# Eight modulation rows and the mixer's sums of squares as TensorE columns, gates by tanh, the mixer's work in new orders

## The chip, the cores and the metric

One core of a Trainium2 chip runs the whole network. The metric is the device time of one execution in microseconds (us), lower is better. Engines are named as in the profile: PE is TensorE (PEld its weight loads), DVE is VectorE, ACT is ScalarE, POOL is GpSimd, SP is the queue that issues DMAs.

## What is computed

Two layers over 512 tokens of width 1024, in float32. Each layer computes six modulation vectors of a conditioning vector `c` (48 rows of 128 results per layer), a mixer (sliding-window attention beside a gated linear recurrence) and a gated feed-forward part (FFN) with a short convolution.

```python
def rg_lru(x, w_a, b_a, w_x, b_x, lam):
    r = sigmoid(einsum('bsnd,nde->bsne', xb, w_a) + b_a)
    i = sigmoid(einsum('bsnd,nde->bsne', xb, w_x) + b_x)
    log_a = -LRU_C * r * softplus(-lam)
    a = exp(log_a)
    b = sqrt(-expm1(2.0 * log_a)) * (i * x)
    _, h = associative_scan(combine, (a, b), axis=1)
    return h

c_act = silu(c)
for l in range(DEPTH):
    mod = (c_act @ ada_w[l] + ada_b[l]).reshape(bsz, N_MOD, D_MODEL)
    shift_m, scale_m, gate_m, shift_f, scale_f, gate_f = ...
    h = rms_norm(x, mix_pre_g[l]) * (1.0 + scale_m) + shift_m
    # mixer: q, k, v, x_lru, gate = split(h @ w_in[l]); attention; rg_lru
    merged = concatenate([rms_norm(attn_out, g_attn), rms_norm(lru_out, g_lru)])
    x = x + gate_m * rms_norm(merged @ w_out[l], mix_post_g[l])
    h = rms_norm(x, ffn_pre_g[l]) * (1.0 + scale_f) + shift_f
    x = x + gate_f * rms_norm(conv_ffn(h, ...), ffn_post_g[l])
```

## The kernel before

Activations lie transposed: 128 features by 512 tokens a tile. Each engine has its own program, written out in order, and they meet at semaphores.

**Weights.** A product with a weight chunk (128 outputs, 1024 inputs, 512 KB) takes three passes: `ACT` copies the raw chunk to its high part `wH` (`split_step`, line 558), DVE subtracts to get the low part `wL` (`lo_chunk`, line 1089), and PE adds up high by high, high by low and low by high (line 1833). Six chunks are held in a ring. A chunk's load is issued on SP (line 430) when PE has finished the chunk six places before (`chunk_done`).

**The in-projection.** The first six chunks of a layer (k, four q, v) are done by token halves in one group (`first_group` in layer 0, `next_group` in layer 1). Chunks 6 to 13 (four x for the recurrence, four gate) follow as `tile_products` of 24 passes on 128x512 each. Between their halves (`midway`) and behind them (`behind`) PE does the attention's and the recurrence's small products: `scores_mm`, `values`, `gates`, `probs_transposed`, `outputs_mm`, each for one of four blocks of tokens or channels.

**The out-projection.** `half_products` with the attention's half of the inputs (chunks O0 to O0+5, both token halves, 12 passes of 128x256 a chunk and half), the norm's statistics, and then the recurrence's half. Attention and recurrence outputs are each normed: `square_out` and `out_squares` (line 1318) square the attention output and sum it over four tiles on DVE, `lru_square` and `lru_sum` (line 1373) do so for the recurrence, and `norm_cols` turns the sums over partitions into columns of a PSUM bank on PE, with the data as weights and a column of ones as the moving operand. `sd_step`, the reciprocals and `norm_spread` make the scale, and `lru_scaled`, `lru_high`, `lru_low` (lines 1527, 758, 1533) apply it before PE can start on the recurrence's half.

**Modulation rows.** A row is a *unit*: a 512 KB tile of `ada_w`, multiplied by the broadcast `csb` and summed along the free axis by one DVE instruction (`dot_unit`, line 1095, counted in `ada_used`). Units 0 to 15 are done before the in-projection, four of them (`PE_SHIFT`) as eight one-column products on PE (`shift_sums`). Units 16 to 23 (`IN_UNITS`, the gate of the mixer) are done by DVE inside layer 0's mixer, units 24 to 39 (`late`) from the end of the mixer through the out-projection, and 40 to 95 in layer 0's FFN, one or two behind a weight chunk's `lo_chunk` (`UNITS`). Their loads are issued by SP (line 444), in one program with the weight loads: for each such unit SP waits until DVE has used the one that lies in its slot, and goes on to the next weight load only then.

```python
if l == 0 and i in UNITS and not NPROJ <= i < FFN0:
    for u in UNITS[i]:
        unit_refill(unit_after(u), u)
```

**Gates.** `gate_sigmoids` (lines 705, 706) uses the sigmoid, `decays` (lines 712, 715) exp and tanh, so ACT loads function tables between them.

The order of the mixer's steps is written out by hand for each engine and layer (the lists from lines 796 on ACT, 1385 on DVE and `midway`/`behind` on PE). An fp32 product of small operands (columns, scores, gates) is one instruction in the program and stands as two rows in the trace.

Of the kernel before, what the change touches and what calls it, by code (L numbers as in the profile page):

```python
# [25 lines left out]
P = 128  # L26
DEPTH, SEQ, D = 2, 512, 1024
# [64 lines left out]
PE_SHIFT = (1, 3, 5, 7)  # L92
SLAB = GRP * P
# [4 lines left out]
def build(nc, A):  # L98
# [3 lines left out]
    with ctx:  # L102
# [51 lines left out]
        tiny = sb("tiny", [P, 132])  # L154
# [33 lines left out]
        presq = [scr[:, :], vwf, work[:, :], gw[:, :, :].rearrange("p a b -> p (a b)")]  # L188
        ada_slots = [stage[:, 10, :], stage[:, 11, :], adaw[:, 0, :], adaw[:, 1, :], vwf]
# [67 lines left out]
        sdx, rsx = tiny[:, 124:128], tiny[:, 128:132]  # L257
        edge = sb("edge", [P, GRP, BACK])
        nil = sb("nil", [P, P], fp32r)
# [9 lines left out]
        ada_used = sem("ada_used")  # L269
        csil_ready, csil_mm, csb_ready = sem("csil_ready"), sem("csil_mm"), sem("csb_ready")  # L270
# [11 lines left out]
        lru_summed = sem("lru_summed")  # L282
# [14 lines left out]
        gate_mm, sig_done, aT_ready, b2_ready = sem("gate_mm"), sem("sig_done"), sem("aT_ready"), sem("b2_ready")  # L297
# [3 lines left out]
        pt_mm, pt_copied, o_mm, o_copied, osq_ready = sem("pt_mm"), sem("pt_copied"), sem("o_mm"), sem("o_copied"), sem("osq_ready")  # L301
# [95 lines left out]
        IN_UNITS = range(2 * KT, 3 * KT)  # L397
        LATE_UNITS = range(3 * KT, DEPTH * NMOD * KT)
# [4 lines left out]
        def unit_fill(u):  # L403

            return sum(1 for v in range(2 * KT, u + 1) if unit_slot(v) == unit_slot(u))

        def unit_after(u):

            return u + 3 if u + 3 < LATE_UNITS.stop else None


        @block.sync
        def _(sp):
# [29 lines left out]
            def ada_fill(u):  # L443
                sp.dma_start(ada_slots[unit_slot(u)], A["ada"][u]).then_inc(ada_in[unit_slot(u)], 16)

            def unit_refill(u, before):

                if u is not None:
                    sp.wait_ge(ada_used, UNIT0 + before - 2 * KT + 1)
                    ada_fill(u)  # L450
# [1920 lines left out]
```

## Time and profile before

| | |
|---|---|
| median of 3 runs | 1223.01 us (1222.08 to 1223.96) |
| the profiled execution: its own time | 1217.96 us |
| its span | 1216.1 us |
| its mean granted TensorE clock | 0.975 |
| PE busy | 1165.7 us, 96% |
| PEld busy | 1010.2 us, 83% |
| DVE busy | 864.0 us, 71% |
| ACT busy | 545.4 us, 45% |
| POOL busy | 13.1 us, 1% |

Times in the trace count from the start of the span. Layer 0's mixer runs from 54 to 205 us, its FFN to 640, layer 1's mixer from there to 791, its FFN to the end. A granted clock of 1.00 is 2.4 GHz, 0.50 is 1.2 GHz. Line numbers in profile rows are those of the kernel before.

### The profile page before, as it was taken

How to read it: one execution, taken by the hardware profiler on the slowest of the kernel's cores; microseconds unless marked ns; L12 is line 12 of the kernel's file. 1: busy time of each engine (PE TensorE's matmuls, PEld its weight loads, DVE VectorE, ACT ScalarE, POOL GpSimd, SP SyncE). 2: the span in 40 equal slices, each digit the busy share in tenths (PEclk: the TensorE clock that was granted, in tenths of full speed). 3: DMA queues.
4: the chain of work that ended last, by engine and by line, in shares of the span. 5: the costliest groups of instructions: out<-in, count | busy, mean ns of one | idle time of the engine just before them, and what ended most of it. 6: DMA issues, size and time to landing. Idle time of an engine off the chain costs nothing.

```text
span 1216.1 us, 16091 instructions
## 1 busy us (share of the span) xinstructions
PE 1165.7 (96%) x6588; PEld 1010.2 (83%) x6588; DVE 864.0 (71%) x1337; ACT 545.4 (45%) x775; POOL 13.1 (1%) x35
## 2 busy tenths in 40 slices
PE   7989888999899999999999999999999999999995
PEld 7977688988788888888999778988888888888895
DVE  8899988778876777777586997478753656346645
ACT  5579634454324431444346894435531444134430
POOL 4000000000000000000000000000000000000000
PEclk8999988999999999999999999989999999999998
DMA  9632547044684448643222221303333323333212
GB/s 359 232 103 71 190 142 240 1 156 164 219 281 166 150 139 268 222 156 111 83 68 89 69 70 53 105 1 123 103 95 96 104 87 104 91 100 103 88 53 70
DMA packets 44937, 155.78 MB, mean 128 GB/s; under 512 B 5056, under 2 KB 7360, under 8 KB 44864
## 3 DMA queue, kind: packets, MB, share of 16 engines
q1 hardware_dynamic: 44720, 154.23, 38.2%
q8 instruction: 52, 0.85, 0.3%
q10 hardware_dynamic: 144, 0.52, 0.1%
q14 instruction: 21, 0.17, 0.0%
HBM read 152.64 MB, written 2.10 MB: 127 GB/s over the span
## 4 chain that ended last, share of the span: by engine, by line
PE 78%; DVE 12%; DMA 4%; ACT 3%; issue 2%; SPq 1%; DVEq 0%
PE ps L1833 77%; DMA sb_stage<-in_ada 2%; DVE sb_wL L1089 2%; DMA sb_raw<-in_w 2%; DVE sb_R L1559 1%; DVE sb_y L1148 1%; ACT sb_R L778 1%; DVE sb_adaw L1095 1%; DVE sb_x L1152 1%; DVE sb_y L1170 1%; DVE sb_y L1358 1%; ACT sb_hH L605 0%; DVE sb_mL L1380 0%; DVE sb_ssqv L1318 0%; DMA sb_vw<-in_ada 0%
## 5 line engine op out<-in xcount | busy, mean ns | idle before, releaser
L1833 PE MATMUL ps<-sb_hH,sb_wH 128*128 128x512 f32 (+1 forms) x1184 | 424.7, 364 | 7.7 <-ACT sb_hH L605 5.2
L1833 PE MATMUL ps<-sb_hH,sb_wL 128*128 128x512 f32 (+1 forms) x1184 | 418.2, 359 | 0.0
L1833 PE MATMUL ps<-sb_hL,sb_wH 128*128 128x512 f32 (+1 forms) x1184 | 395.1, 358 | 2.7 <-DVE sb_hL L1177 2.7
L1833 PEld LDWEIGHTS ps<-sb_hH,sb_wH 128*128 128x128 f32 x1184 | 228.8, 193 | 43.5 <-ACT sb_hH L605 6.0
L1833 PEld LDWEIGHTS ps<-sb_hH,sb_wL 128*128 128x128 f32 x1184 | 228.7, 193 | 31.7
L1833 PEld LDWEIGHTS ps<-sb_hL,sb_wH 128*128 128x128 f32 x1184 | 214.0, 192 | 35.5 <-DVE sb_hL L1177 3.3
L558 ACT ACTIVATE sb_wH<-sb_raw 128x1024 fp32r<-128x1024 f32 x174 | 181.5, 1050 | 138.3 <-DMA sb_raw<-in_w 138.1
L1089 DVE TENSOR_TENSOR sb_wL<-sb_raw,sb_wH 128x1024 fp32r<-128x1024 f32 x174 | 211.4, 1219 | 38.3 <-ACT sb_wH L558 38.1
L1833 PE MATMUL ps<-sb_mH,sb_wH 128*128 128x256 f32 (+1 forms) x608 | 207.0, 341 | 3.7 <-ACT sb_mH L992 3.5
L1833 PE MATMUL ps<-sb_mL,sb_wH 128*128 128x256 f32 (+1 forms) x608 | 205.9, 339 | 1.7 <-DVE sb_mL L1533 1.7
L1833 PE MATMUL ps<-sb_mH,sb_wL 128*128 128x256 f32 (+1 forms) x608 | 205.3, 338 | 0.0
L1833 PEld LDWEIGHTS ps<-sb_mH,sb_wH 128*128 128x128 f32 x608 | 118.2, 194 | 16.5 <-ACT sb_mH L992 4.0
L1833 PEld LDWEIGHTS ps<-sb_mL,sb_wH 128*128 128x128 f32 x608 | 118.2, 194 | 14.8 <-DVE sb_mL L1533 2.5
L1684 DVE SCALAR_TENSOR_TENSOR sb_R<-ps,sb_par,sb_R 128x511 f32<-128x511 f32 x84 | 62.9, 748 | 94.9 <-ACT sb_R L986 94.8
L1833 PEld LDWEIGHTS ps<-sb_mH,sb_wL 128*128 128x128 f32 x608 | 118.2, 194 | 11.4
L986 ACT ACTIVATE sb_R<-ps,sb_par 128x512 f32<-128x512 f32 x84 | 65.2, 776 | 103.9 <-PE ps L1833 103.9
L992 ACT ACTIVATE sb_mH<-sb_I 128x512 fp32r<-128x512 f32 x42 | 26.5, 632 | 100.7 <-DVE sb_I L1694 100.7
L1687 DVE SCALAR_TENSOR_TENSOR sb_R<-ps,sb_par,sb_R 128x510 f32<-128x510 f32 x84 | 62.9, 748 | 3.0
L1095 DVE SCALAR_TENSOR_TENSOR sb_adaw<-sb_adaw,sb_csb 128x1024 f32<-128x1024 f32 x48 | 57.9, 1219 | 4.9 <-DMA sb_adaw<-in_ada 4.5
L1696 DVE TENSOR_TENSOR sb_mL<-sb_I,sb_mH 128x512 fp32r<-128x512 f32 x42 | 29.1, 692 | 29.3 <-ACT sb_mH L992 29.3
L982 ACT ACTIVATE sb_I<-sb_R 128x512 f32<-128x512 f32 x42 | 26.6, 632 | 49.1 <-DVE sb_R L1687 49.1
L605 ACT ACTIVATE sb_hH<-sb_y,sb_mod 128x256 fp32r<-128x256 f32 x48 | 22.8, 503 | 28.1 <-DVE sb_y L1170 28.0
(223 smaller groups left out, 1098.3 us busy)
## 6 DMA issues: line engine op xcount, KB each, us to landing
sb_raw<-in_w SPq DMA_DIRECT2D x174, 512.0 KB, 3.7
sb_adaw<-in_ada SPq DMA_DIRECT2D x48, 512.0 KB, 4.4
sb_stage<-in_ada SPq DMA_DIRECT2D x24, 512.0 KB, 11.2
sb_vw<-in_ada SPq DMA_DIRECT2D x24, 512.0 KB, 4.6
sb_side<-in_w SPq DMA_DIRECT2D x8, 512.0 KB, 4.9
sb_raw<-in_w SPq DMA_DIRECT2D x8, 384.0 KB, 14.6
sb_x<-in_x SPq DMA_DIRECT2D x4, 512.0 KB, 5.3
out<-sb_x SPq DMA_DIRECT2D x4, 512.0 KB, 2.9
```

Of the source, the lines that this page charges most:

```text
L558: nc.scalar.activation(high_of(n), raw_of(n), ACT.Copy).then_inc(w_hi, 1)
L605: nc.scalar.activation(hH[:, j, part_of(h)], yt(j)[:, part_of(h)], ACT.Identity, bias=bias[:, j:j + 1], scale=1.0).then_inc(hi_ready, 1)
L778: last = nc.scalar.activation(R[:, c % 4, part_of(h)], pair_bank(h, p)[:, (c % 2) * HALF:(c % 2 + 1) * HALF], ACT.Identity, bias=pcol(l, " ...
L982: nc.scalar.activation(I[:, p % 2, :], R[:, (c - 1) % 4, :], ACT.Gelu_apprx_tanh).then_inc(f_gelu, 1)
L986: nc.scalar.activation(R[:, c % 4, :], bank(up_bank(u)), ACT.Identity, bias=par_l[:, COLS["fcb"] + col:COLS["fcb"] + col + 1], scale=pcol( ...
L992: nc.scalar.activation(mH[:, p, :], I[:, 2 + p % 2, :], ACT.Copy).then_inc(act_hi, 1)
L1089: TT(low_of(n), raw_of(n), high_of(n).bitcast(fp32), ALU.subtract).then_inc(w_lo, 1)
L1095: STT(out=tile, in0=tile, scalar=1.0, in1=csb[:, :], op0=ALU.mult, op1=ALU.mult, accum_out=mod[:, seg, kt:kt + 1]).then_inc(ada_used, 1)
L1684: link(STT(out=buf[:, 1:], in0=acc[:, 0:SEQ - 1], scalar=pcol(l, "fcw", 2 * PAIRS + col), in1=buf[:, 1:], op0=ALU.mult, op1=ALU.add))
L1687: STT(out=buf[:, 2:], in0=acc[:, 0:SEQ - 2], scalar=pcol(l, "fcw", col), in1=buf[:, 2:], op0=ALU.mult, op1=ALU.add).then_inc(f_taps, 1)
L1696: TT(mL[:, p, :], I[:, 2 + p % 2, :], mH[:, p, :].bitcast(fp32), ALU.subtract).then_inc(act_lo, 1)
L1833: return nc.tensor.matmul(out, a, b, start=start, stop=stop, **kw)
```

## The change

- **Units 16 to 23 on PE** (`EARLY`, `unit_sums`): 64 one-column products in layer 0's mixer, two units ahead of `scores_mm(0)` and six behind `values(0)`. Their tiles go to eight slots of the staging area by loads that SP issues before weight chunks 6 and 8; bank 7 holds the sums, and `in_tile(7, 0)` waits until DVE has read them (`gate_mod`).
- **Other unit loads from POOL.** SP issues weight loads alone from there; units 24 to 95 are issued on POOL's queue. Units 24 to 31 are done by DVE inside the mixer, so that eight instead of ten units remain for the out-projection (`late(8, 2)`, `late(10, 2)`).
- **Sums of squares as columns** (`attn_cols`, `lru_cols`): 32 one-column products a layer instead of 8, adding up in one bank; `out_squares` and `lru_sum` are gone. Squares of the attention output get four buffers (`sqo`).
- **Gates by tanh**: `gate_tanhs` with scale 0.5, the constants of `decays`, `root` and `gated` adapted.
- **Orders**: `midway` and `behind` give way to a list of half tiles (`in_tile`), small products, columns and `attn_products`, and ACT's and DVE's lists are new for both layers. The ropes of layer 1's second half move from the tail of layer 0's list to the head of layer 1's.

```diff
+        EARLY = range(2 * KT, 3 * KT)
+        early_slots = [stage[:, s, :] for s in (0, 1, 4, 5, 10, 11, 12, 13)]
...
@@ sync
-            for n in range(GRP, GRP + 4):
-                refill(n)
+            sp.wait_ge(ada_used, 2)
+            early_fill(0)
+            early_fill(1)
+            sp.wait_ge(ada_used, 5)
+            early_fill(2)
+            early_fill(3)
+            refill(GRP)
+            refill(GRP + 1)
+            sp.wait_ge(ada_used, 9)
             sp.wait_ge(shift_mm, 3)
-            sp.wait_ge(ada_used, 9)
-            ada_fill(IN_UNITS[0])
-            ada_fill(IN_UNITS[1])
-            for n in range(GRP + 4, 2 * GRP):
+            early_fill(4)
+            early_fill(5)
+            sp.wait_ge(ada_used, 11)
+            early_fill(6)
+            early_fill(7)
+            for n in range(GRP + 2, 2 * GRP):
                 refill(n)
...
-                    if l == 0 and i in UNITS and not NPROJ <= i < FFN0:
-                        for u in UNITS[i]:
-                            unit_refill(unit_after(u), u)
...
@@ gpsimd
+            def ada_fill(u):
+                nc.gpsimd.dma_start(ada_slots[unit_slot(u)], A["ada"][u]).then_inc(ada_in[unit_slot(u)], 16)
...
+            pool.wait_ge(o_mm, QT)
+            for u in LATE_UNITS[:3]:
+                ada_fill(u)
+            for u in LATE_UNITS[3:]:
+                pool.wait_ge(ada_used, unit_used(u - 3))
+                ada_fill(u)
...
@@ scalar
-                    nc.scalar.activation(R[:, j, :], bank(ba), ACT.Sigmoid, bias=pcol(l, "ba", j))
+                    S.mark(nc.scalar.activation(R[:, j, :], bank(ba), ACT.Tanh, bias=bias2[:, l, j:j + 1], scale=0.5))
...
-                    nc.scalar.activation(sq[:, :], bank(O_BANK), ACT.Square).then_inc(o_copied, 1)
+                    nc.scalar.activation(sqo[t], bank(O_BANK), ACT.Square).then_inc(o_squared, 1)
...
@@ vector
-                def out_squares(t):
...
-                def lru_sum(j):
...
+                def gate_mod():
+
+                    dve.wait_ge(unit_mm, PE_UNITS)
+                    link(TT(mod[:, 2, 0:PE_UNITS], bank(7)[:, 16:16 + PE_UNITS], bias_col(2, 0, PE_UNITS), ALU.add))
+                    dve.sem_inc(gate_read, 1)
...
-                late(6, 3)
+                late(8, 2)
                 add_square(l, 0, 0, 0)
-                late(9, 3)
+                late(10, 2)
...
@@ tensor
+            def unit_sums(i):
+
+                pe.wait_ge(unit_in[i], 16)
+                for k in range(KT):
+                    last = mm(bank(7)[:, 16 + i:17 + i], early_slots[i][:, k * P:(k + 1) * P], csil[:, k:k + 1],
+                              k == 0, k == KT - 1)
+                last.then_inc(unit_mm, 1)
...
+                def attn_cols(t, final=False):
+
+                    pe.wait_ge(o_squared, l * QT + t + 1)
+                    for j in range(AT):
+                        last = mm(bank(6)[:, t:t + 1], sqo[t][:, j * P:(j + 1) * P], ones[:, 0:1], False,
+                                  final and j == AT - 1)
...
+                def lru_cols(j, final=False):
...
                 if l == 0:
                     first_group()
+                    in_tile(6, 0)
+                    unit_sums(0)
+                    unit_sums(1)
+                    scores_mm(0)
+                    in_tile(6, 1)
+                    values(0)
+                    unit_sums(2)
+                    unit_sums(3)
+                    unit_sums(4)
+                    unit_sums(5)
+                    unit_sums(6)
+                    unit_sums(7)
+                    scores_mm(1)
+                    in_tile(7, 0)
+                    in_tile(7, 1)
...
+                    attn_cols(1)
+                    attn_cols(2)
+                    lru_cols(0)
+                    attn_products(0, 2)
+                    outputs_mm(3)
+                    lru_cols(1)
+                    attn_products(0, 3)
+                    lru_cols(2)
+                    attn_cols(3)
+                    attn_products(0, 4)
+                    lru_cols(3, True)
+                    attn_products(0, 5)
+                    attn_products(1, 0)
+                    norm_spread(1 + l, 7, ratio)
+                    attn_products(1, 1)
...
```

The first place is PE in layer 0's mixer, behind the second half of x chunk 6 (`sb_ident,sb_ssqv` is `values(0)`, `sb_kd,sb_y` a `scores_mm`, `sb_tiny,sb_stage` unit columns). Before:

```order
L1833 MATMUL ps<-sb_hH,sb_wH 128x512
L1833 MATMUL ps<-sb_hL,sb_wH 128x512
L1833 MATMUL ps<-sb_hH,sb_wL 128x512
L2058 MATMUL ps<-sb_ident,sb_ssqv 128x128 x4
L1833 MATMUL ps<-sb_hH,sb_wH 128x512
```

and now:

```order
L1841 MATMUL ps<-sb_hH,sb_wH 128x512
L1841 MATMUL ps<-sb_hL,sb_wH 128x512
L1841 MATMUL ps<-sb_hH,sb_wL 128x512
L2069 MATMUL ps<-sb_ident,sb_ssqv 128x128 x4
L1841 MATMUL ps<-sb_tiny,sb_stage 128x1 x48
L1841 MATMUL ps<-sb_kd,sb_y 64x128 x16
L1841 MATMUL ps<-sb_hH,sb_wH 128x512
```

Between `values(0)` and chunk 7 there are now 48 one-column products in a row and the second block's scores.

The second place is PE in layer 0's out-projection, where the norm's columns are summed (`sb_ones` is the moving operand). Before:

```order
L1833 MATMUL ps<-sb_mL,sb_wH 128x256
L1833 MATMUL ps<-sb_mH,sb_wL 128x256
L1833 MATMUL ps<-sb_ones,sb_I 128x1 x4
L1833 MATMUL ps<-sb_ones,sb_ssqv 128x1 x4
L1833 MATMUL ps<-sb_mH,sb_wH 128x256
```

and now, at the first of the places where columns stand together:

```order
L1841 MATMUL ps<-sb_mL,sb_wH 128x256
L1841 MATMUL ps<-sb_mH,sb_wL 128x256
L1841 MATMUL ps<-sb_ones,sb_sqo_89 128x1 x4
L1841 MATMUL ps<-sb_ones,sb_sq 128x1 x4
L1841 MATMUL ps<-sb_ones,sb_I 128x1 x4
L1841 MATMUL ps<-sb_nil 128x512
L1841 MATMUL ps<-sb_mH,sb_wH 128x256
```

Eight products in one place have become 32 in six places, 12 of them together here.

The third place is SP's queue behind the first loads (`sb_raw` are weight chunks, `sb_stage`, `sb_adaw` and `sb_vw` units). Before:

```order
L430 DMA sb_raw<-in_w 128x1024 x4
L444 DMA sb_stage<-in_ada 128x1024 x2
L430 DMA sb_raw<-in_w 128x1024 x3
L444 DMA sb_stage<-in_ada 128x1024
L430 DMA sb_raw<-in_w 128x1024 x3
```

and now:

```order
L451 DMA sb_stage<-in_ada 128x1024 x4
L437 DMA sb_raw<-in_w 128x1024 x2
L451 DMA sb_stage<-in_ada 128x1024 x4
L437 DMA sb_raw<-in_w 128x1024 x12
L437 DMA sb_side_60<-in_w 128x1024
```

Eight unit loads stand ahead of the weight chunks, and behind them SP issues weights alone.

## Rows read from the trace of the kernel before

**Rows 1.** The page, part 1: busy time by engine, share of the span, instructions.
```profile
PE 1165.7 (96%) x6588; PEld 1010.2 (83%) x6588; DVE 864.0 (71%) x1337; ACT 545.4 (45%) x775; POOL 13.1 (1%) x35
```

**Rows 2.** Busy us of each engine by stretch, then granted clock, DMA share, GB/s.
```profile
135.00:160.00 25.00, 17.98 (x126) 16.75 (x124) 23.26 (x36) 8.12 (x14) 0.00 (x0) 0.86 0.47 177
680.00:720.00 40.00, 40.00 (x222) 29.62 (x221) 38.89 (x60) 36.44 (x49) 0.00 (x0) 1.00 0.19 58
```

**Rows 3.** Who PE waited for, 62 to 175 us: total, times, longest.
```profile
PE ps L1833 <- DVE sb_mL L1380: 4.7, 1, 4.7
...
PE ps L2084 <- DVE sb_mL L1380: 0.3, 1, 0.3
```

**Rows 4.** Stretches of layer 0's mixer at the low clock, columns as in group 2.
```profile
69.50:72.91 3.41, 3.41 (x18) 2.58 (x13) 3.24 (x7) 2.82 (x5) 0.00 (x0) 0.51 0.00 0
148.00:154.80 6.80, 5.20 (x23) 5.14 (x24) 6.80 (x12) 1.42 (x3) 0.00 (x0) 0.50 0.04 15
161.65:168.50 6.85, 6.26 (x29) 6.00 (x28) 4.70 (x12) 0.00 (x0) 0.00 (x0) 0.50 0.83 295
```

**Rows 5.** Timeline of PE, a unit's columns at full clock: start, us, instruction.
```profile
50.27 1.84 PE L1833 MATMUL ps<-sb_tiny,sb_stage 128*128 128x1 f32 x16
51.98 0.36 PE L1833 MATMUL ps<-sb_hL,sb_wH 128*128 128x256 f32 x1
```

**Rows 6.** Timeline of PE, a unit's last columns at the low clock.
```profile
18.53 1.42 PE L1833 MATMUL ps<-sb_tiny,sb_stage 128*128 128x1 f32 x6
19.81 0.56 PE L1833 MATMUL ps<-sb_hH,sb_wH 128*128 128x256 f32 x1
```

**Rows 7.** Timeline of PE, sixteen columns behind a short wait.
```profile
641.43 2.17 PE L1833 MATMUL ps<-sb_ones,sb_R 128*128 128x1 f32 x16 [0.36 <-DVE sb_R L1157]
```

**Rows 8.** Stretch with group 7's columns, the one behind it, one around group 5's.
```profile
639.50:642.90 3.40, 3.04 (x27) 2.84 (x26) 2.49 (x4) 1.06 (x1) 0.00 (x0) 1.00 0.00 0
642.90:646.30 3.40, 3.40 (x18) 3.40 (x18) 0.24 (x2) 0.26 (x1) 0.00 (x0) 0.51 0.02 5
...
49.02:55.84 6.82, 6.76 (x58) 6.58 (x58) 5.92 (x10) 2.64 (x4) 0.00 (x0) 1.00 0.17 37
```

**Rows 9.** Who PE waited for, 660 to 760 us.
```profile
PE ps L1833 <- DVEq L1514: 0.8, 1, 0.8
PE ps L2084 <- DVE sb_mL L1380: 0.7, 1, 0.7
```

**Rows 10.** Layer 1's low-clock stretch behind the norm's columns, as in group 2.
```profile
748.70:752.20 3.50, 3.50 (x17) 3.41 (x17) 0.44 (x3) 0.27 (x1) 0.00 (x0) 0.52 0.00 0
```

**Rows 11.** The chain of waits, 277 to 291 us: start, us, what.
```profile
278.49 0.33 SPq L444
...
278.86 6.45 DMA sb_raw<-in_w
...
285.33 1.07 ACT sb_wH L558
...
286.42 1.22 DVE sb_wL L1089
287.65 2.30 DVE sb_adaw L1095 x4
...
289.96 0.33 SPq L444
```

**Rows 12.** PE at layer 0's first down chunk, the stretch behind, and a dense one.
```profile
317.02 0.50 PE L1833 MATMUL ps<-sb_mH,sb_wH 128*128 128x512 f32 x1 [3.53 <-ACT sb_mH L992]
...
318.70:322.10 3.40, 3.40 (x10) 2.64 (x9) 3.33 (x6) 0.17 (x1) 0.00 (x0) 0.50 0.23 35
...
400.00:440.00 40.00, 40.00 (x178) 33.14 (x177) 27.70 (x36) 16.92 (x22) 0.00 (x0) 1.00 0.45 151
```

**Rows 13.** A group by line and shape, then a DMA issue: count, KB each, median us to landing.
```profile
L1340 DVE TENSOR_SCALAR sb_Adec<-sb_R 128x512 f32<-128x512 f32 x8 | 3.4, 427 | 0.3
...
sb_adaw<-in_ada SPq DMA_DIRECT2D x48, 512.0 KB, 4.4
```

More of the change, by code:

```diff
@@ L92 @@
 PE_SHIFT = (1, 3, 5, 7)
+PE_UNITS = 8
 SLAB = GRP * P
@@ L153, in build @@
         ssq = ssqv[:, 0:SEQ]
-        tiny = sb("tiny", [P, 132])
+        tiny = sb("tiny", [P, 128])
         spl = sb("spl", [P, DEPTH, LT])
@@ L269, in build @@
         ada_used = sem("ada_used")
+        unit_in = [sem(f"unit_in{i}") for i in range(KT)]
+        unit_mm, gate_read = sem("unit_mm"), sem("gate_read")
         csil_ready, csil_mm, csb_ready = sem("csil_ready"), sem("csil_mm"), sem("csb_ready")
@@ L403, in unit_fill, with unit_used @@
         def unit_fill(u):
-            return sum(1 for v in range(2 * KT, u + 1) if unit_slot(v) == unit_slot(u))
-        def unit_after(u):
-            return u + 3 if u + 3 < LATE_UNITS.stop else None
+            return sum(1 for v in range(3 * KT, u + 1) if unit_slot(v) == unit_slot(u))
+        def unit_used(u):
+            return UNIT0 + u - FIRST_DVE + 1
         @block.sync
@@ L909, in _ @@
                     lru_square(3)
-                sd_step(1 + l, bank(6), D_ATTN, 2)
-                for j in range(LT):
-                    lru_high(j)
+                    sd_step(1 + l, bank(6), D_ATTN, 2)
+                    lru_high(0)
+                    lru_high(1)
+                    lru_high(2)
+                    lru_high(3)
                 split_step(O0 + 6)
@@ new lines, in in_tile @@
+                def in_tile(i, part):
+                    if part == 0:
+                        pe.wait_ge(w_lo, w_no(B + i))
+                        if l == 0 and i == GRP + 1:
+                            pe.wait_ge(gate_read, 1)
+                        if i >= GRP + 2:
+                            if i - 2 < FIRST_G:
+                                pe.wait_ge(taps_done, l * LT + i - 2 - FIRST_X + 1)
+                            else:
+                                pe.wait_ge(g_copied, l * LT + i - 2 - FIRST_G + 1)
+                    acc = bank(in_bank(i))
+                    for kt in range(part * KT // 2, (part + 1) * KT // 2):
+                        a, al = block_pair(B + i, kt)
+                        mm(acc, a, hH[:, kt, :], kt == 0, False)
+                        mm(acc, a, hL[:, kt, :], False, False)
+                        last = mm(acc, al, hH[:, kt, :], False, kt == KT - 1)
+                    if part:
+                        last.then_inc(chunk_done, 1)
@@ new lines, in _ @@
+                    values(0)
+                    in_tile(6, 0)
+                    in_tile(6, 1)
+                    in_tile(7, 0)
+                    in_tile(7, 1)
+                    values(1)
+                    scores_mm(1)
+                    gates(0)
+                    in_tile(8, 0)
+                    in_tile(8, 1)
+                    gates(1)
+                    in_tile(9, 0)
+                    in_tile(9, 1)
+                    gates(2)
+                    probs_transposed(0)
@@ new lines, in _ @@
+                    scores_mm(2)
+                    in_tile(10, 0)
+                    outputs_mm(0)
+                    in_tile(10, 1)
+                    gates(3)
+                    scores_mm(3)
+                    probs_transposed(1)
+                    in_tile(11, 0)
+                    outputs_mm(1)
+                    in_tile(11, 1)
+                    in_tile(12, 0)
+                    in_tile(12, 1)
+                    probs_transposed(2)
+                    in_tile(13, 0)
@@ L2328 @@
         ada[kt] = blocks[:, :, 0, kt, :].transpose(1, 0, 2).reshape(P, D)
+    for kt in range(PE_UNITS):
+        ada[2 * KT + kt] = blocks[:, :, 2, kt, :].transpose(1, 0, 2).reshape(P, D)
     gw = np.zeros((L, P, 2 * LT, P), np.float32)
```

723 lines of the change are left out of this document (351 added, 372 removed).

## The prediction

> **What bounds the kernel now.** I read the page first: PE is busy for 1165.7 of 1216.1 us, DVE for 864.0 [rows 1]. So a change gains only what PE now loses, in waits or at the low clock, and anything added on PE counts in full unless it fills a wait. Then the busy times by stretch, to see where PE loses: from 135 to 160 us it is busy for 17.98 of 25 while DVE works for 23.26 [rows 2], so layer 0's mixer is held up by DVE there. In layer 1's mixer (680 to 720) DVE is as full, 38.89 of 40, yet PE is busy for all 40 [rows 2]: there PE itself is the bound. The table of waits gives the size: in layer 0's mixer PE waits ten times, 12.7 us in all, the longest 4.7 for the low part of the attention output [rows 3]. The granted clock adds to that. It stands at its low level, 1.2 instead of 2.4 GHz, in three stretches of that mixer, in which PE is busy for 3.41, 5.20 and 6.26 us [rows 4], and half of such time is lost.
>
> **The modulation units on PE.** One product is two rows of the trace. A unit is eight products, 16 passes, and takes 1.71 us at full clock, from 50.27 to 51.98 [rows 5], 0.107 us a pass. Eight units are 13.7 us more on PE. They take eight instructions of about 1.2 us off DVE, which is what PE waited for, and units 0 and 1 stand where PE now waits 3.1 us for the rope ahead of `scores_mm(0)`. Bounds of the eight: 13.7 us if the clock stays up, and 8 x 16 x 0.213 = 27.3 us if it is down throughout; 0.213 is the pace of the last six passes of the first unit, (19.81 - 18.53) / 6, at the low clock [rows 6].
>
> **What the clock does with 96 passes in a row.** No row shows more than about 2 us of columns together. Where 16 stood behind a wait of 0.36 us, the clock was at 1.00 with them and at 0.51 in the stretch behind, 642.9 to 646.3 [rows 7, 8]. Where 16 stood in the midst of dense products (50.27), it stayed at 1.00, to 55.84 [rows 5, 8]. Columns hardly keep the array at work, so I take it that they count with the waits and not with the products, and that six units, 10.3 us without one wide product, bring the clock down. I let it fall about halfway, after 44 passes (4.7 us); the other 52 cost 52 x (0.213 - 0.107) = 5.5 us more, and the products behind run at half pace for one low stretch as long as those in the rows, 3.4 us, of which 1.7 are lost. Together 7.2 us, near the middle of the bounds, which are 0 (it never falls) and 96 x 0.106 + 3.4 = 13.6 us (it is down from the start, and for a stretch of 6.8 us behind). The low stretch at 69.5 [rows 4] I leave where it is: what it follows changes from a wait to columns.
> The Trainium skill ("TensorE: Matmul & The Clock Gate", section "HAM oscillation — how this bites in real kernels") puts the low clock down to gaps in which TensorE is idle. By that rule units without a gap between them cost nothing beyond their 13.7 us; it is the first rival below.
>
> **Sums as columns.** Each layer gets 32 products for 8, so 48 passes more: 48 x 0.107 = 5.1 us of PE. From DVE go four `out_squares` and three `lru_sum`. In layer 0 three column groups stand together, 24 passes or 2.6 us, more than the 16 that brought the clock down in rows 7; one low stretch of 3.4 us costs 1.7 us. Bounds 0 and 3.4 us (two such stretches). In layer 1 the clock falls behind the 16 columns now as well (748.7 to 752.2 [rows 10]), so nothing is added for it.
>
> **What comes back in the mixers.** In layer 0 DVE loses seven units ahead of `lru_low`, 1.15 us each (2.30 for two [rows 11]), and with them the seven sums: over 8 us of work, and its program no longer stands between PE and each of its waits. The new order also puts the scaling of the recurrence's output behind the first product of the second token half, so that the products of five chunks cover it. I take all 12.7 us of waits as gone, and the two later low stretches with them: (5.20 + 6.26) / 2 = 5.7 us. The bounds are half of both, 9.2, and all of it, 18.4; I take the upper end, since the new lists start each product on what DVE and ACT finished a step or more before. What is late next is PE itself. In layer 1 the waits are 0.8 and 0.7 us [rows 9]; both go.
> Tanh for the sigmoid spares ACT table loads and `root` gets a scale. ACT is not what PE waits for in these rows but for 0.8 us, already counted, so this is nothing; it stands beside PE's products and would count only if ACT were late.
>
> **The queues.** In layer 0's FFN the chain from 277 to 291 us runs in a ring: SP issues unit loads, then a weight load of 6.45 us, ACT splits (1.07), DVE subtracts (1.22), DVE does units (2.30), and only then SP goes on [rows 11]. One turn is 289.96 - 278.49 = 11.5 us for two weight chunks, and PE needs 48 passes of 40 / 178 = 0.225 us, 10.8 us, for them. PE eats up its lead and waits 3.53 us at 317.02, and then runs at the low clock for 3.40 us [rows 12]. With the unit loads on POOL, SP waits for PE alone, and the ring is cut. Layer 1, with no units, has no such wait at its place. Gain 3.5 + 1.7 = 5.2 us. Bounds: 5.2, and 0 if POOL's loads bring the delay back. In layer 0's start eight unit loads, 4.2 MB, go ahead of weight chunks 6 and 8. The DMA engines are busy for 0.17 of the time from 49.02 to 55.84 us [rows 8], when ACT begins on those chunks, so there is room; I take nothing, with 2 us as the upper bound. Two units fewer in the out-projection, where PE does not wait: nothing.
> What POOL adds is a price that no row shows, since POOL issues nothing here; the nearest row is SP's, 4.4 us to landing [rows 13]. An estimate by the Trainium skill ("DMA: Bandwidth & Descriptors", section "Anatomy of one DMA — SWDGE (gpsimd) path") is 2.0 us + bytes / 436e3, 3.2 us for 512 KB, which leaves the sum as it is.
>
> **The sum.** Layer 0's mixer: +13.7 +7.2 +5.1 +1.7 -12.7 -5.7 = +9.3 us. Layer 1's mixer: +5.1 -1.5 = +3.6. Layer 0's FFN: -5.2. Together +7.7 us. The sum stands on the profiled execution, which took 1217.96 us, so that one would take 1225.7. The median of the runs is 1223.01, 5 us above it, without another reading of where; on that basis I predict **1230.7 us**.
>
> **Rivals.**
> *Columns keep the clock up* (faster). Then the 7.2 and 1.7 us fall away, and so do the low stretches behind columns that I left in place, half of 3.41 and of 3.50 us: -12.3, so 1218.4 us. It decides at the point where PE has done some 5 us of unit columns: passes at 0.107 us there or at 0.213. For it speaks that each fall in the rows has a wait nearby too, as the skill's rule has it; against it, that the waits were as short as 0.36 us. Chance 0.22.
> *The mixer hid more than its waits.* Stretched passes around the table loads, the openings of banks and single small waits within "busy" go as well when DVE and ACT have air, some 5 us, or half of the unit block's clock loss. 1222 to 1225.5 us, chance 0.16.
> *POOL's loads come late* (slower still). In layer 0's down chunks DVE does two units per 5.5 us with three slots, so a load may take about 8 us from the use of its slot. At 10 us each three units would take nearly 2 us longer, some 10 us over 32 or so of them, and the FFN's 5.2 don't come: above 1237 us. A rule of the Trainium skill ("SBUF — State Buffer", section "Who interferes with whom") points this way: loads issued from GpSimd starve while DVE runs two-port operations. By the row, DVE has one such operation in the mixer, 128x512 in 427 ns, eight times [rows 13], and none in the FFN. Chance 0.10.
> *It does what it says, as summed*: 1226 to 1237 us, chance 0.52.
>
> **How the numbers follow.** The range 1218.4 to 1237.5 us takes in the first rival at its own time and the bounds of the clock's and the waits' terms short of their far ends; the rest is left out on both sides. About 0.2% (2.4 us) is what a measurement of this kernel can tell from no change. Faster by more than that is most of the first rival and a little of the second: 0.22. Within it is the second rival's upper part and the first's slow end: 0.14. Slower: 0.64.
>
> **What would show it.** Right: PE's granted clock at 0.5 within the six units of layer 0's mixer, about 5 us into them, and no PE wait above 1 us from there to the end of the mixer; the first products of the recurrence's half start some 9 us later than now; layer 1's mixer 3 to 4 us longer with DVE no longer full; no wait at the first down chunk of layer 0, and weight loads every 5.5 us in the FFN. Wrong: a granted clock of 1.00 through the units, DVE waiting for unit loads, PE waiting for `gate_read`, weight chunks 7 to 9 late on ACT, or new waits of PE on ACT's lists, which have been made anew.

## The result, and the profile after

| | before | changed |
|---|---|---|
| median of 20 runs | 1221.97 us (1219.43 to 1224.44) | 1226.86 us (1222.51 to 1232.59) |
| the profiled execution: its own time | 1217.96 us | 1229.81 us |
| its span, its mean granted clock | 1216.1 us, 0.975 | 1228.0 us, 0.969 |

The changed kernel takes 1.0043 times as long, with a 95% interval of 1.0028 to 1.0057: 4.9 us slower. 7.7 us was forecast. The two profiled executions lie further apart than the medians, 11.9 us, since the one of before is below its own median and the one of the change above; a second profile of each stands in experiment 9. The verdicts go by the medians.

The page of the changed kernel, busy time by engine (to [rows 1]):

```profile
PE 1194.6 (97%) x6814; PEld 1042.4 (85%) x6814; DVE 843.0 (69%) x1307; ACT 526.0 (43%) x760; POOL 50.7 (4%) x108
```

PE has 28.9 us more, DVE 21.0 less. Between common marks (the starts of instructions that both kernels have) the spans compare so:

| stretch | before | changed | difference |
|---|---|---|---|
| to chunk 6 | 62.42 | 63.38 | +1.0 |
| layer 0's mixer, to the FFN's first norm | 142.5 | 157.5 | +15.0 |
| layer 0's FFN, to the next layer's columns | 436.5 | 431.8 | -4.7 |
| to layer 1's mixer | 17.3 | 15.7 | -1.5 |
| layer 1's mixer | 132.5 | 134.3 | +1.8 |
| layer 1's FFN and the end | 424.9 | 425.3 | +0.4 |

Windows of the changed kernel: the DVE-bound piece of before, the six units up to the fall of the clock and the low stretch from there, and the low stretch at the columns of layer 0's out-projection (columns as in [rows 2]):

```profile
135.00:160.00 25.00, 25.00 (x144) 21.45 (x143) 24.22 (x38) 19.73 (x26) 0.00 (x0) 0.98 0.38 127
...
76.09:80.42 4.33, 4.33 (x42) 4.33 (x40) 4.22 (x8) 2.98 (x4) 0.00 (x0) 1.00 0.42 121
80.42:97.49 17.07, 17.07 (x95) 16.34 (x95) 4.96 (x11) 0.00 (x0) 1.29 (x2) 0.50 0.19 62
158.93:176.00 17.07, 17.07 (x78) 15.54 (x77) 4.74 (x8) 4.19 (x10) 1.56 (x3) 0.50 0.27 92
```

From 135 to 160 us PE was busy for 17.98 of 25 [rows 2] and is now for all 25. In the whole mixer, 63 to 200 us, it has no wait that the table shows. What it does instead is run at half clock: the six units begin at 76.09 us at 1.00, the clock falls at 80.42, 39 passes into the 96, and stays at 0.50 for 17.1 us with PE busy for every bit of it. It falls again at 158.93, about 20 passes into the 24 column passes that stand together, for another 17.1 us. A third low stretch, 3.4 us from 70.2, stands behind the 32 passes of units 0 and 1. Before, the mixer had 14.9 us of PE work at the low clock [rows 4]; now it has 37.6. DVE and ACT have hardly anything to do in the stretch at 158.93 (4.74 and 4.19 us).

The timeline of PE, a late unit at the low clock, and the first down chunk of layer 0's FFN:

```profile
90.78 1.85 PE L1841 MATMUL ps<-sb_tiny,sb_stage 128*128 128x1 f32 x8
92.55 2.89 PE L1841 MATMUL ps<-sb_kd,sb_y 64*64 64x128 f32 x32
...
329.82 0.50 PE L1841 MATMUL ps<-sb_mH,sb_wH 128*128 128x512 f32 x1 [0.60 <-ACT sb_mH L1011]
```

(92.55 - 90.78) / 8 is 0.22 us a pass, twice the full-clock pace. The down chunk waits 0.60 us instead of 3.53 [rows 12], with no low stretch behind it. POOL's loads, from the page:

```profile
sb_adaw<-in_ada POOLq DMA_DIRECT2D x44, 512.0 KB, 4.8
```

4.8 us to landing, against 4.4 from SP [rows 13].

### The profile page after: what moved, and what is told of

It reads as the page before. It is cut to its first block, busy times and chain, and to the rows that moved or that the text cites. A ratio compares the mean times of both kernels' runs of the same rounds, so it can differ in the third digit from the quotient of the medians.

```text
span 1228.0 us, 16492 instructions
## 1 busy us (share of the span) xinstructions
PE 1194.6 (97%) x6814; PEld 1042.4 (85%) x6814; DVE 843.0 (69%) x1307; ACT 526.0 (43%) x760; POOL 50.7 (4%) x108
## 4 chain that ended last, share of the span: by engine, by line
PE 85%; DVE 9%; ACT 3%; issue 1%; DMA 0%; SPq 0%; DVEq 0%
PE ps L1841 85%; DVE sb_wL L1103 1%; DVE sb_R L1572 1%; DVE sb_y L1167 1%; ACT sb_R L786 1%; DVE sb_R L1700 1%; DVE sb_x L1171 1%; PE ps L2095 1%; DVE sb_R L1697 1%; DVE sb_y L1189 1%; DVE sb_adaw L1109 0%; ACT sb_hH L615 0%; ACT sb_R L1005 0%; ACT sb_wH L568 0%; DVE sb_I L1587 0%
## 5 line engine op out<-in xcount | busy, mean ns | idle before, releaser
L1109 DVE SCALAR_TENSOR_TENSOR sb_adaw<-sb_adaw,sb_csb 128x1024 f32<-128x1024 f32 x44 | 53.5, 1220 | 8.9 <-DMA sb_adaw<-in_ada 8.6
L536 POOL DMA_DIRECT2D sb_adaw<-in_ada x44 | 23.2, 528 | 281.2 <-DVE sb_adaw L1109 250.9
## 6 DMA issues: line engine op xcount, KB each, us to landing
sb_stage<-in_ada SPq DMA_DIRECT2D x24, 512.0 KB, 14.1
```

What stands on the lines that cost most here:

```text
L536: nc.gpsimd.dma_start(ada_slots[unit_slot(u)], A["ada"][u]).then_inc(ada_in[unit_slot(u)], 16)
L1109: STT(out=tile, in0=tile, scalar=1.0, in1=csb[:, :], op0=ALU.mult, op1=ALU.mult, accum_out=mod[:, seg, kt:kt + 1]).then_inc(ada_used, 1)
```

## The experiments

Times are medians against the kernel before in the same series; its own median was between 1221.3 and 1221.7 us in each. An edit of the kernel before is called so; all others are edits of the changed kernel.

**1. The loads alone** (`pool_loads`, kernel before).

```diff
-            def ada_fill(u):
-                sp.dma_start(ada_slots[unit_slot(u)], A["ada"][u]).then_inc(ada_in[unit_slot(u)], 16)
...
+            def ada_fill(u):
+                nc.gpsimd.dma_start(ada_slots[unit_slot(u)], A["ada"][u]).then_inc(ada_in[unit_slot(u)], 16)
...
+            pool.wait_ge(shift_mm, 3)
+            pool.wait_ge(ada_used, 9)
+            for u in IN_UNITS[:2]:
+                ada_fill(u)
...
```

> The kernel before with one part of the change: all unit loads behind the start are issued on POOL instead of SP, with the same waits for their slots. Theory A (SP's ring through DVE's units delays weight chunks): the wait of 3.53 us at the first down chunk of layer 0 goes, with the low clock behind it, 5.2 us, and the median is 5 us below the kernel before, 1217. Rival B (the gain in the FFN came with the order of the mixer, which hands the FFN its chunks at another time): the wait stays, within 1 us of before. Rival C (POOL's loads starve or come late): DVE waits for sb_adaw above 20 us in all, and slower than before.

1211.81 us against 1221.35, ratio 0.9918 (0.9905 to 0.9932): 9.5 us gained, more than the FFN holds. In its profile layer 0's FFN takes 432.0 us instead of 436.5 (the wait is 0.59 us), and the mixer 140.6 instead of 142.5, or instead of 144.7 in the second profile of before (experiment 9). DVE's timeline at the head of the mixer, of the kernel before and of this one:

```profile
59.82 1.22 DVE L1095 SCALAR_TENSOR_TENSOR sb_stage<-sb_stage,sb_csb 128x1024 f32<-128x1024 f32 x1 [4.47 <-DMA sb_stage<-in_ada]
```

```profile
55.88 1.16 DVE L1079 SCALAR_TENSOR_TENSOR sb_stage<-sb_stage,sb_csb 128x1024 f32<-128x1024 f32 x1
...
58.46 0.69 DVE L1244 TENSOR_TENSOR sb_R<-ps,sb_cosT 128x512 f32<-128x512 f32 x1 [1.41 <-ACT sb_sq L648]
```

Before, DVE stood 4.47 us for unit 16's tile, which SP issues behind the loads of chunks 6 to 9 and their waits for `group_kt`; the rope behind it was late, and PE waited 3.1 us for it ahead of `scores_mm(0)`. From POOL the tile is there, PE's wait is 0.35 us, and the low clock at 69.5 us is gone. Not all of that stays gained, since other waits grow: from 62 to 200 us PE still waits 10.9 us in all (12.7 before), and its low stretches in the mixer make 17.1 us, as many as in the first profile of before and 3.4 fewer than in the second. Theory A is right in the FFN and misses half of the gain.

**2. Loads back to SP** (`sp_loads`). The same refills in SP's program, in their places between the weights.

> The changed kernel with its unit loads 24 to 95 issued by SP again, in one program with the weights as in the kernel before; all else as changed. Theory A (the change holds two parts of opposite sign, POOL's loads about -9.5 us as measured alone, and the mixer's new work about +14): the wait at layer 0's first down chunk comes back with 3.5 us, the stretch from layer 0's FFN tiles to the next layer's columns takes 387 us instead of 383, and the median is 5 to 9 us above the changed kernel, 1232 to 1236. Rival B (POOL's loads gained only where unit 16 stood at the head of DVE's mixer list, and the new order has no such place): the median stays within 2 us of the changed kernel's 1227.

1255.99 us, ratio 1.0288: far above what either theory gave. Where PE loses it in the mixer (100 to 200 us), and whom DVE waits for:

```profile
DVE sb_stage L1122 <- DMA sb_stage<-in_ada: 26.5, 5, 9.2
...
PE ps L1854 <- ACT sb_xc L706: 10.6, 1, 10.6
...
ACT sb_xc L706 <- DVE sb_I L1372: 9.2, 1, 9.2
```

DVE stands for unit tiles that SP issues only after its waits for chunks, ACT for DVE, and PE for ACT. This says how much one queue for both costs in the new order with the loads where I put them, and not what POOL's loads are worth in the change. Only its FFN can be used: 438.0 us and a wait of 4.3 us at the down chunk, against 431.8 and 0.60, so 6 us there.

**3. Units back on DVE** (`units_dve`).

```diff
-PE_UNITS = 8
+PE_UNITS = 0
```

with `mod_unit(16)` to `mod_unit(23)` in DVE's list, units 24 to 39 behind them as in the kernel before, and the loads of all of them from POOL.

> The changed kernel with the eight units of the first gate back on DVE in the mixer (in the places in DVE's list where it has units 24 to 29), units 24 to 39 behind it as in the kernel before; the new orders, the columns, tanh and POOL's loads stay. Theory A (DVE was what PE waited for in layer 0's mixer, and the units on PE cost 13.7 us and about 7 of low clock): PE loses its 20 us of columns and half clock, and gets waits back, 12 us if the new lists bring nothing, none if they alone do: -16 to -4 us against the changed kernel, so -11 to +1 against the one before. Rival B (the lists cannot bear DVE's units: PE waits longer than before): PE waits in layer 0's mixer of over 15 us, and slower than the kernel before.

1215.58 us, ratio 0.9954 (0.994 to 0.9968), 5.8 below before, so about 11 below the change. PE loses 20 us of columns and gets these waits (63 to 200 us):

```profile
PE ps L1824 <- DVE sb_adaw L1299: 3.1, 1, 3.1
PE ps L1824 <- DVEq L1592: 2.9, 1, 2.9
PE ps L1824 <- DVE sb_tiny L1137: 2.4, 1, 2.4
PE ps L1824 <- DVE sb_work L1299: 1.6, 1, 1.6
```

With the new orders PE's ten waits, 12.7 us in all, have become four, 10.0 us. Against `pool_loads` it is 3.8 us slower: orders, columns and tanh together have not paid for themselves here, though two of the waits (2.9 at 188.4 and 2.4 at 193.8) stand behind late units, whose places in DVE's list I chose: DVE stands 3.67 us for the tile of the one that it begins at 191.97.

**4. Units spread** (`units_spread`).

```diff
-                    in_tile(6, 0)
-                    unit_sums(0)
-                    unit_sums(1)
+                    in_tile(6, 0, (4,))
                     scores_mm(0)
-                    in_tile(6, 1)
+                    unit_sums(5)
+                    in_tile(6, 1, (6,))
                     values(0)
-                    unit_sums(2)
-                    unit_sums(3)
-                    unit_sums(4)
-                    unit_sums(5)
-                    unit_sums(6)
                     unit_sums(7)
```

and units 0 to 3 in `first_group`.

> The changed kernel with its eight units of columns one by one among wide products: units 0 to 3 in the tail of the first group, 4 and 6 inside the halves of tile 6, 5 and 7 behind scores_mm(0) and values(0). The number of columns is the same. Theory A (a long run of one-column products brings the clock down by itself): no low clock of about 17 us behind values(0), a unit takes 1.71 us wherever it stands, and the profiled run ends about 7 us sooner than the changed kernel's 1228.0 us span, some 1221; the median goes from +4.9 us against the kernel before to about 0. Rival B (the clock falls there for another reason, the waits and small products of the score blocks, or at random): the low stretch stays within that part of the mixer and the median stays at +4 to +6 us. Rival C (spread columns weigh the array down in the first group as well): low clock from 55 us on, and slower than the changed kernel.

1216.69 us, ratio 0.9963 (0.995 to 0.9976): 9.6 us better than the change by the two differences, with the same instructions in another order. Its windows over all eight units and the stretch behind:

```profile
52.80:76.70 23.90, 23.84 (x194) 22.89 (x192) 13.99 (x23) 18.40 (x31) 0.75 (x1) 1.00 0.29 97
76.70:89.55 12.85, 11.92 (x130) 10.96 (x130) 8.68 (x16) 4.73 (x7) 0.54 (x1) 1.00 0.39 124
89.55:92.96 3.41, 3.41 (x9) 2.67 (x10) 3.31 (x5) 0.00 (x0) 0.00 (x0) 0.50 0.00 0
```

Each unit takes 1.70 us, most of them between wide products of 1.5 to 4 us, and the clock stays at 1.00 to 89.5. Theory A, and more than it had: the low stretch at 70 us went too, since units 0 and 1 no longer stand together ahead of `scores_mm(0)`, and from 50 us to the end of the mixer 6.8 us at the low clock are left, against 37.6 in the change.

**5. The run in another place** (`units_block`): the eight units in one run behind the first group.

> The changed kernel with all eight units in one run of 128 passes directly behind the first group, ahead of tile 6, where PE has had 20 us of dense wide products and neither a wait nor the small products of scores_mm stand near; behind the run come tile 6, scores_mm(0) and the rest without units. Theory A (a long run of columns brings the clock down wherever it stands): the granted clock falls some 4 to 5 us into the run, near 68 us, and stays at 0.5 for the rest of it and more, 10 to 17 us in all; the units take 22 to 24 us instead of 13.7, and the median is within 3 us of the changed kernel's 1227. Rival B (the place: score blocks and small waits bring it down, the columns are only what follows): the clock stays at 1.00 through the run, the units take 13.7 us, and the median is 1217 to 1220, as units_spread.

1232.00 us, ratio 1.0088. The run begins at 62.53 us:

```profile
53.00:62.53 9.53, 9.47 (x80) 9.29 (x79) 7.61 (x12) 8.78 (x13) 0.00 (x0) 1.00 0.30 99
62.53:66.24 3.71, 3.71 (x36) 3.71 (x35) 3.29 (x6) 3.58 (x9) 0.00 (x0) 1.00 0.64 211
66.24:90.14 23.90, 23.90 (x105) 23.13 (x105) 2.05 (x4) 7.14 (x13) 1.29 (x2) 0.50 0.16 56
```

The clock falls 3.7 us into it and is down for 23.9 us. Ahead of it there is no wait and no score block, only wide products (PE is busy for 9.47 of the last 9.53 us), with one unit of 16 passes at 50.38. The units take 23.77 us. It is the run of columns, in both places where it was tried. The time is above the 1224 to 1230 us that theory A had, and the profile shows two things that it left out: PE waits 3.8 us at 101.6 for `gate_read`, and 20.5 us more at the low clock follow, from 100.4 and from 168.6.

**6. Dummy products between** (`units_wide`).

```diff
+                    for _ in range(4):
+                        mm(bank(7)[:, HALF:SEQ], nil[:, :], nil[:, 0:1].broadcast_to([P, HALF]), True, True)
```

> The changed kernel with the six units where they stand behind values(0), and four dummy products of 128x256 (zeros, written to a part of bank 7 that nobody reads, about 0.5 us together) between each two of them: 20 passes more, 2.4 us. Theory A (a run of columns without wide products brings the clock down, at any place in the program): the passes go on at 0.107 us, there is no low stretch of 17 us at 80 to 97, and the median is 4 to 7 us below the changed kernel, 1220 to 1223. Rival B (it was the place, the waits and the scores around it, and units_spread gained by moving): the clock falls as before, the median is 2.4 to 4 us above the changed kernel, 1229 to 1231. Rival C (half a microsecond of wide products for 1.7 of columns is not enough): a shorter or later fall, within 2 us of 1227.

1228.67 us, ratio 1.007: nothing saved.

```profile
77.83:83.47 5.64, 5.64 (x54) 5.64 (x52) 3.71 (x7) 2.98 (x4) 0.00 (x0) 1.00 0.32 93
83.47:103.95 20.48, 20.48 (x108) 19.36 (x108) 6.16 (x10) 0.54 (x2) 1.29 (x2) 0.50 0.17 52
```

The clock falls 5.6 us behind the start of the units, where the changed kernel's two profiles have 4.3 and 5.4 us (experiment 9), so not even a delay is shown, and then it stays down for 20.5 us. Half a microsecond of wide products per unit saves nothing: rival C in its time, but the fall is not a shorter one. They were products of zeros, so whether real data would do more was not tried.

**7. Columns spread** (`cols_spread`), at most eight passes in a row, and **8. both** (`both_spread`).

```diff
...
                     attn_cols(1)
+                    attn_products(0, 1, 1)
+                    attn_products(0, 2, 0)
                     attn_cols(2)
+                    attn_products(0, 2, 1)
+                    outputs_mm(3)
+                    attn_products(0, 3, 0)
                     lru_cols(0)
-                    attn_products(0, 2)
-                    outputs_mm(3)
+                    attn_products(0, 3, 1)
...
```

> The changed kernel with the norm's column groups of layer 0's out-projection one by one among half products of the attention's chunks, at most eight passes in a row instead of 24. Theory A: the low clock from 158.4 to 175.5 us, 17.1 us long, goes, and the recurrence's half starts 8 us sooner (at 177 instead of 185.2 us); the median goes from +4.9 us against the kernel before to about -3. Rival B (share of columns in the stretch counts, not their run): the clock falls all the same and nothing is gained, +4 to +6 us. Rival C (with the clock up PE catches up with DVE and ACT, which then set the start of the recurrence's half): waits for sb_mL or sb_mH at its start, and only 2 to 4 us gained.

> The changed kernel with both spreadings, the eight units of columns and the norm's column groups. If the two add up: units_spread stood at 1216.7 us with one low stretch of 3.4 us left in the out-projection (153.8 to 157.2), which is 1.7 us; so 1215 us and no low clock between 93 and 200 us. If the columns' total share of a stretch counts and not their run: the low stretch is there all the same, 1216.7.

1223.76 us, ratio 1.0020 (1.0009 to 1.0031), and 1216.93 us, ratio 0.9973. In the profile of `cols_spread` the low stretch of the out-projection is gone:

```profile
158.00:175.00 17.00, 17.00 (x144) 16.27 (x143) 9.39 (x18) 6.58 (x14) 2.09 (x4) 1.00 0.32 111
```

Its median gains 2.5 us, not 8. In `both_spread` the clock stays up from 91.6 to 206 us, as expected, but the median is not the 1215 us expected: on top of spread units, spread columns bring no gain that can be told. Experiment 9 shows why.

**9. Both kernels once more** (`after_again`, `before_again`).

> The changed kernel once more, unchanged, for another profile: its 20 runs lie in two groups, about 1223.5 us at a mean granted clock of 0.975 and about 1230 at 0.970. If the groups differ by how long one of the two low stretches of 17.1 us lasts (80 to 97, 158 to 175), a profile of the short kind shows one of them at 3.4 or 6.8 us and all other pieces as in the profile at hand; if by DMA or waits, the low stretches are the same and a wait differs. A profile of the long kind again settles nothing but shows whether the stretches stand at the same places.

> The kernel before once more, unchanged, for a second profile. The one shown took 1217.96 us, 4 to 5 us below the median of its runs. If that gap is in the granted clock, a run near the median shows a longer low stretch or one more in layer 0's mixer than the three of 3.4, 6.8 and 6.9 us, and the waits of 3.1 us ahead of scores_mm(0) and 3.5 us at the first down chunk stand as they were. If it is in DMA or waits, the low stretches are the same and a wait or the start differs by 4 us.

1227.38 and 1220.25 us. The changed kernel's second profile (1227.32 us):

```profile
77.30:82.72 5.42, 5.42 (x52) 5.42 (x50) 3.89 (x7) 2.98 (x4) 0.00 (x0) 1.00 0.34 97
82.72:99.79 17.07, 17.07 (x91) 15.85 (x91) 6.59 (x10) 0.97 (x2) 1.30 (x2) 0.50 0.22 62
161.23:164.64 3.41, 3.41 (x18) 2.41 (x16) 2.60 (x3) 0.42 (x1) 0.00 (x0) 0.50 0.00 0
```

The stretch in the units is there again, 17.1 us, and begins 5.4 us into the six units, behind 49 passes. The one in the out-projection is 3.4 us this time, though the work is the same, and the one at 70 us is 6.8 instead of 3.4. The other kernels with the same 24 passes together show 3.4 us there (`units_dve`, `units_spread`, `units_wide`) or 13.7 (`units_block`, `sp_loads`). So what spreading the columns saves changes from run to run; 3.4 us is what most profiles have, and the first profile of the change shows the dearest form. By stretch, all four profiles:

| stretch | before | once more | changed | once more |
|---|---|---|---|---|
| layer 0's mixer | 142.5 | 144.7 | 157.5 | 152.7 |
| layer 0's FFN | 436.5 | 437.7 | 431.8 | 432.1 |
| to layer 1's mixer | 17.3 | 15.7 | 15.7 | 17.3 |
| layer 1's mixer | 132.5 | 131.0 | 134.3 | 134.3 |
| layer 1's FFN and the end | 424.9 | 424.9 | 425.3 | 426.1 |
| own time | 1217.96 | 1219.62 | 1229.81 | 1227.32 |

What is the same in both columns of a kernel is the kernel's: the mixers, and the FFN's gain, +8 to +15, +1.8 to +3.3 and -4.4 to -5.9 us. The 1.5 us ahead of layer 1's mixer come and go in both kernels with a low stretch there; so do the 1.5 in layer 1's mixer of the kernel before, where the second profile has none at the columns ([rows 10] has). The run times follow the mean clock: in the changed kernel 0.976 at 1222.51 us and 0.968 at 1232.59, in the one before 0.975 at 1219.30 and 0.969 at 1223.01. The waits of before, 3.15 and 3.88 us, are there again (3.10 and 3.53 in the first profile), and its mixer has one low stretch of 3.4 us more. `pool_loads` is 1.9 us shorter in the mixer and 4.5 in the FFN than the first profile of before, 4.1 and 5.7 than the second; the last two are near the 9.5 us of the medians.

**10. Versions meant to beat both** (`best1`, `best2`).

> A version meant to beat both: the changed kernel with no unit on PE (units 16 to 23 on DVE, as in units_dve), PE's list in layer 0 with scores_mm(1) and scores_mm(2) one half tile later, the fourth block's probabilities transposed ahead of tile 13 so that the late units' loads can start 10 us sooner, and the column groups spread. From units_dve (1215.6 us, profiled span 1217.2): its four waits of 1.58, 3.12, 2.88 and 2.40 us and the low stretches behind them (3.4, 6.8, 6.8 us long in the mixer, half lost) are 10 + 8.5 us; if all go, 1198; if DVE is late elsewhere for half of that, 1206; if DVE's list is simply full, 1212 as pool_loads or above.

> best1 with its two faults mended: gated(3) directly behind gated(2), since ACT stood 6.9 us for it ahead of the last block's squares and PE then 3.9 us for them, and products of the second token half (1,0), (1,1) between the recurrence's column groups, which otherwise stand among half products at the low clock from 144 to 165 us. If these two were what kept best1 at 1214.3: no wait above 1 us between 63 and 205 us, the recurrence's half starts near 160 instead of 170.5 us, and the median is 1204 to 1207. If DVE's list is simply full (it works without a gap to 149 us): waits for lru_square or for the scaled outputs of 2 to 4 us, and 1209 to 1212.

`best1` took 1214.27 us. It reached the out-projection 5 us before `units_dve`, and then PE waited 3.9 us for `lru_square`, the clock fell, and it stayed down while column groups stood between half products:

```profile
144.20:164.70 20.50, 18.70 (x85) 18.51 (x86) 11.53 (x21) 4.75 (x11) 2.12 (x4) 0.51 0.20 60
```

`best2` moves `gated(3)` and puts whole products between the groups. 1207.54 us, ratio 0.9882 (0.987 to 0.9895), 14 us below the kernel before. PE's waits from 63 to 200 us, the longest 1.5, and windows of the whole stretch:

```profile
PE ps L1824 <- DVE sb_xc L1318: 1.7, 2, 1.1
PE ps L1824 <- DVEq L1592: 1.5, 1, 1.5
...
PE ps L2078 <- DVE sb_mL L1366: 0.4, 1, 0.4
```

```profile
63.00:110.00 47.00, 44.92 (x306) 33.28 (x305) 44.64 (x72) 34.04 (x59) 1.58 (x3) 1.00 0.31 101
110.00:150.00 40.00, 39.93 (x251) 33.97 (x250) 39.41 (x65) 27.05 (x40) 3.15 (x6) 1.00 0.46 158
150.00:197.00 47.00, 44.46 (x363) 43.31 (x361) 37.99 (x68) 18.56 (x29) 8.44 (x16) 1.00 0.67 237
```

It has the change's columns, tanh, POOL loads and most of its orders, with the units on DVE. The clock is 1.00 throughout; the next low stretch, 6.8 us from 197.8, lies behind the mixer, where the kernel before has one too (206.1). It gains 14.1 us where `pool_loads` gains 9.5, so orders that cost 3.8 us in `units_dve` pay once the long waits are out and the column groups have whole products between them. The two repairs were not tried apart.

## Why the prediction came out as it did

The direction was right, and the size within its range; the parts were not all right.

**Units on PE, and the clock in them: right, slightly low.** The clock was to fall after 44 passes and did after 39 in the first profile and 49 in the second. In the first, the 12.1 us of units at the low clock, 0.213 us a pass, cost 6.1, and 4.9 us more at the low clock behind them cost 2.5: together half of 17.1, 8.5 us against 7.2. Experiments 4 and 5 show that it is the run of columns. The first rival is out: that columns keep the clock up fails at 0.22 us a pass. The Trainium skill's account ("TensorE: Matmul & The Clock Gate", section "HAM oscillation — how this bites in real kernels"), idle gaps, does not cover this: up to the fall PE was busy for 4.33 of 4.33 us in the change and for 3.71 of 3.71 in `units_block`. The rival's time was nevertheless to be had, by spreading.

**Columns of the norm in layer 0: right in most profiles, with too narrow a bound.** I had one low stretch of 3.4 us, 1.7 lost, and at most two. The second profile has just that, and so have three other kernels with the same columns; the first has 17.1 us, 8.5 lost, and two others 13.7. I took the length from [rows 8], where dense products followed. Here more groups follow, 2.6 to 4.6 us apart, but they follow in the second profile too, where the clock came back after 3.4 us. So why it stays down longer in one execution than in another is open. In the first profile the low clock made the mixer (37.6 - 14.9) / 2 = 11.4 us dearer, against 3.2 forecast (7.2 + 1.7 - 5.7).

**The waits: right in sum; what stood behind one of them was the step that failed.** All 12.7 us are gone. But the 3.1 us ahead of `scores_mm(0)` were not DVE's load of work, as I had it: DVE stood 4.47 us for unit 16's tile, which came late in SP's queue. `pool_loads` leaves the unit on DVE, and the wait is 0.35 us all the same. In the change, taking the unit out of DVE's list removes the same wait, at the price of the columns on PE. I read the rope as late and did not follow it to its first wait, and no term of the sum has the price of that queue in the mixer, which is 1.9 us against one profile of before and 4.1 against the other. The low stretch at 69.5 I left in place, and it is in place, behind columns now: 3.4 us in the first profile and 6.8 in the second.

With 13.7 us of units, 5.1 of columns, 11.4 of clock and 12.7 of waits the mixer of the first profile sums to +17.5, and +15.0 was measured. The other 2.5 us I cannot place; stretched passes around DVE's and ACT's delays, as in the second rival, would be of that size, but no experiment shows them. The forecast was +9.3, the second pair of profiles has +8.0. The second pair has 27.3 us of PE work at the low clock against 17.9, so most of the way from +15.0 to +8.0 is in how long these stretches last.

**Layer 0's FFN: right.** -5.2 forecast, -4.4 to -5.9 measured. The wait fell by 2.9 us (3.53 to 0.60), not by all 3.5, and the low stretch behind it went. The third rival is out: DVE waits 8.6 us for `sb_adaw` over the FFN, 2.3 at most, and PE does not wait for that. The Trainium skill's estimate for such a load ("DMA: Bandwidth & Descriptors", section "Anatomy of one DMA — SWDGE (gpsimd) path"), 3.2 us, is short of the measured 4.8.

**Layer 1's mixer: right.** +3.6 forecast; +3.3 against the profile of before that has no low stretch there, +1.8 against the other. The two waits went. Sixteen passes at a time, with products between and no wait, leave the clock at 1.00 over that mixer in both profiles of the change.

**From profile to median.** I added 5 us because the profiled execution of before lay that far below its median. On the profile's basis 1225.7 was forecast and 1229.8 came, 4 too low; on the median's, 1230.7 against 1226.9, 4 too high. Since the run times follow the mean clock (experiment 9), the offset most likely belonged to where that one execution's low stretches had fallen; it did not carry over to another kernel. Both profiles of before are below its median and both of the change above, so which stretches fill the 2.8 us between the forecast +7.7 and the measured +4.9 stays open. That the second pair of profiled executions lies just 7.7 us apart (1219.62 and 1227.32) is in part luck: its mixers are 8.0 apart instead of 9.3, layer 1's mixers 3.3 instead of 3.6, the FFNs -5.6 instead of -5.2, and the stretches for which the sum has no term add another 2.0.

By the medians, along the one path over `pool_loads` and `units_dve`, the change is made of about -9.5 for the loads, +3.8 for orders, columns and tanh (of which some is my own placing in `units_dve`), and +11 for the units on PE. Columns and tanh were not tried alone.

## What to carry to other kernels

Products with one column cost PE more than their own time: many in a row bring the clock down though PE never idles, and it then stays down through the work behind. Spread them: here 16 passes at a time, 1.7 us, between wide products of 1.5 to 4 us kept the clock up, and 0.5 us of wide products between them did not. Check the granted clock of the stretch behind them, in more than one profile. When an engine is late at a mark, follow it back to its first wait: here that ended at a load queued behind others' waits on the same queue, and giving these loads a queue of their own gained 9.5 us, while moving the eight units' work from engine to engine lost 11.

## What was not expected of the hardware

- The granted clock falls 3.7 to 5.4 us into a run of one-column products with PE busy throughout, and stays low for 17.1 to 23.9 us (experiment 5, and both profiles of the change).
- The same program shows 17.1 us at the low clock in one execution and 3.4 in another, at the columns of layer 0's out-projection.
